# Half of the tokens' turns and squares moved out of a router stage into the matrix product ahead of it

## The chip, the cores and the metric

One NeuronCore of a Trainium2 chip runs the whole program. The metric is the device time of one execution in microseconds (us), as the median of several runs. The engines are named as in the profile: PE (matrix products and transposes through the 128x128 array), PEld (its weight loads), DVE, ACT, POOL and SP, which only issues transfers here.

## The reference

Two model blocks in fp32 for one sequence of 512 tokens behind 16 meta tokens, 528 rows of 1024 columns in all. What matters here is the end of the first block's attention and the routing of its mixture of experts:

```python
mixed = concat(attn, conv)                       # 528 x 1024
h = h + mixed @ w_out                            # "second output product": columns 512 to 1023
hs = rms_norm(h, ffn_norm_g)                     # needs the mean square of each row of h
logits = hs @ w_router                           # 16 experts
aff = softmax(logits)
g, idx = top_k(aff.T, 66)                        # each expert takes its 66 best tokens
y = experts(hs[idx])                             # w_gate, w_up, w_down: 384 MB of weights
h = h.at[idx].add(y * g)
```

The program goes on with a second block of two layers, which the change doesn't touch.

## The kernel before

The program is a row of stages. Each is one block in which every engine has its own instruction list, in order; semaphores order the lists among each other, and all engines meet at the stage's end. Three stages matter.

**The first layer's stage** (`first_layer_stage`) ends with the output product, `out`, a `SplitGemm` of 16 steps (0 to 15). Each step takes 128 rows of `w_out`; steps 0 to 7 make columns 0 to 511 of h, steps 8 to 15 columns 512 to 1023. ACT rounds a weight tile and an activation tile to their high parts (`highs`, L482), DVE subtracts them to get the low parts (`lows`, L495), and PE makes 12 matmuls a step (L429): four tiles of tokens times three products of parts. DVE then adds the four result banks to h (L1320). The fifth tile of tokens has only 16 rows (`tail`); its product runs apart (L986, after steps 7 and 11). Into the same lists are woven, by dictionaries that say "after step s do this", the normalising and turning of the memory rows (`memory_rows`: PE L1473 after steps 6, 8, 10, 12). On PE the last of these follows step 12, and steps 13 to 15 follow without anything between.

**The router stage** (`router_stage`) takes h, five tiles of tokens (`TILES1`: four of 128, one of 16). On PE, `turn(t)` transposes a tile in eight pieces (L1638), `parts(t)` multiplies the turned tile with the weights `gained_w` in 16 narrow matmuls (L1653), and `logits(t)` adds up four partial sums with the table `pick` that POOL makes at the stage's start (L1608 to 1612, L1663). The order on PE is turn(0), then for each t: turn(t+1), logits(t-1), parts(t); ahead of logits(3) stands step 0 of another product, `g` (the memory keys, `mem0`, 16 steps of six matmuls, L429). DVE copies every turned half tile from PSUM (`evict`, L1759) and every partial sum (`take_parts`, L1764), then makes the scaled logits and the softmax (L1772 to 1787) and the choice of 66 tokens (L1790 to 1821). ACT squares h (L1710), takes the root of the sums (L1719), makes the high parts of `g` (`high_of`, L1374), the exponential (L1723), and the normalised rows (`normed`, L1725), which SP stores. POOL makes the low parts of `g` (L1387, a TENSOR_TENSOR on 128x512), and then gathers the first expert's rows (L1622). In `g`'s list on PE, the turned scores (L1670) stand behind step 2 and the turned picks (L1683) behind step 10.

**The experts' stage** multiplies 384 pieces of weights of 1 MB each.

The root, and the exponential that waits for DVE's shifted logits, stand in ACT's list like this:

```python
nc.scalar.activation(ss[:, 1, :], ss[:, 0, :], ACT.Sqrt, ...)   # L1719
for i in range(2, NS): g.high_of(act, i)                        # NS = 6
act.wait_ge(s["shifted"], 1)
nc.scalar.activation(aff[:], aff[:], ACT.Exp)                   # L1723
```

Of the kernel before, what the change touches and what calls it, by code (L numbers as in the profile page):

```python
# [23 lines left out]
P = 128  # L24
D = 1024
# [651 lines left out]

def first_layer_stage(m, tok, hn, qk, v, raw, turns, rot_work, kept, slots, late_slots, mixed, names, at, start_at, scales_at,
                      out_slots, load_early, beside):
# [127 lines left out]
    out_on_tensor, out_on_scalar, out_on_vector = beside  # L807
# [3 lines left out]
    with nc.Block() as block:  # L811
# [25 lines left out]
        def _(pe):  # L837
# [160 lines left out]
            work.setdefault(11, []).append(lambda: tail_products(1))  # L998
            out.products(pe, work, start=3)

        @block.scalar
        def _(act):
# [76 lines left out]
            out.split("act", act, out_on_scalar(act), start=2)  # L1079

        @block.vector
        def _(dve):
# [166 lines left out]
            work = out_on_vector(dve)  # L1249
            work.setdefault(10, []).append(lambda: take_tail(0))  # L1250
# [198 lines left out]
def memory_rows(m, mem_x, mem_split, at):  # L1449
# [70 lines left out]
    return load, on_tensor, on_scalar, on_vector  # L1520
# [12 lines left out]
def router_stage(m, h, w, w_loaded, mem_split, mk_rows, mv, ht, normed, small, slots, first_rows, xg):  # L1533
# [9 lines left out]
    slot = (0, 2, 1, 3, 5)  # L1543
# [26 lines left out]
    junk = m.at("router_junk", [P, D], m.gaps[0])  # L1570
    gained_w = m.area("router_w_gained", [P, KD, 32], 90624)
    PART = (7, 3)
    names = ("w_gained cleared squared root inverse normed turned evicted parts parts_taken tables logits shifted exped "
# [19 lines left out]
    with nc.Block() as block:  # L1593
# [35 lines left out]
        def _(pe):  # L1629
            def turn(t):  # L1630
                n = TILES1[t][1]
                for half in range(2):
                    u = 2 * t + half
                    if u >= 3:
                        pe.wait_ge(s["evicted"], u - 2)
                    for k in range(4):
                        f = 4 * half + k
                        ins = pe.transpose(ps[:, 4 + u % 3, k * P:k * P + n], h[0:n, t, f * P:(f + 1) * P],  # L1638
                                           m.ident[0:n, 0:n])
                    ins.then_inc(s["turned"], 1)  # L1640

            def parts(t):

                t0, n = TILES1[t]
                pe.wait_ge(s["evicted"], 2 * t + 2)
# [4 lines left out]
                for half in range(2):  # L1650
                    for q in range(4):
                        k = 4 * half + q
                        ins = pe.matmul(ps[32 * q:32 * q + 32, PART[t % 2], 0:n], gained_w[:, k, :], ht[:, k, t0:t0 + n],  # L1653
                                        start=(half == 0), stop=(half == 1))
                ins.then_inc(s["parts"], 1)

            def logits(t):
# [3 lines left out]
                if t == 0:  # L1661
                    pe.wait_ge(s["tables"], 1)
                pe.matmul(ps[0:n, 2, slot[t] * NE:(slot[t] + 1) * NE], part[:, t0:t0 + n], pick[:, 0:NE], start=True,  # L1663
# [2287 lines left out]
```

## Time and profile before

| | before |
|---|---|
| median of 3 runs | 2188.51 us (2188.34 to 2189.64) |
| the profiled execution's own time | 2187.14 us |
| its span in the profile | 2185.0 us |
| PE busy | 2156.6 us (99%) |
| DVE, ACT, POOL busy | 1653.7, 1391.6, 337.4 us |
| output product, steps 8 to 15 and what runs beside them | about 238.8 to 265.3 us of the span |
| router stage | 265.8 to about 300.5 us |
| experts' stage | 300.5 to about 1388 us |

The span is what the profile shows of the execution; 2.1 us of the execution's own time lie around it. A matmul's row shows its time from first column to end, and the next one begins before that end, so the distance from start to start is what counts on PE. A `[1.20 <-PEq L811]` behind a row says that the engine sat idle for 1.20 us before it, and what ended that.

### The profile page before, as it was taken

The page shows a single profiled execution, that of the slowest core. Times are in us where ns is not written, and L with a number is a line of the kernel's source. Part 1 is how long each engine was busy: PE and PEld are TensorE (multiplying, and loading weights), DVE is VectorE, ACT ScalarE, POOL GpSimd, SP SyncE. Part 2 cuts the span into 40 slices and gives each one's busy share as a digit, 9 for nine tenths or more (in the row PEclk, how much of TensorE's full clock was granted, in tenths as well). Part 3 has the DMA queues.
Part 4 walks back from the last instruction along what each step waited for, and adds up shares of the span by engine and source line. Part 5 has one row for each costly group of instructions (what it writes and reads, how often), then busy time and mean ns, then how long its engine had stood idle before and what let it go on. Part 6 is the DMA issues. An engine that isn't in the chain of part 4 may idle for free. (4 is left out here: it accounts for less than half of the span.)

```text
span 2185.0 us, 31915 instructions
## 1 busy us (share of the span) xinstructions
PE 2156.6 (99%) x11509; PEld 1556.7 (71%) x11509; DVE 1653.7 (76%) x2157; ACT 1391.6 (64%) x1795; POOL 337.4 (15%) x207
## 2 busy tenths in 40 slices
PE   9999999999999999999999999999999999999999
PEld 9988765565565555555555555687797788888777
DVE  6466678998989989899898898756655556875664
ACT  5345577777777777767777777755555555776653
POOL 3032041211122111121121200330000000211000
PEclk9999999999999999999999999999999999999999
DMA  6213479999999999999999999532221131241301
GB/s 189 84 55 121 166 272 371 376 382 371 387 378 375 381 372 382 386 376 374 373 385 383 374 380 369 207 97 77 83 73 58 58 117 53 61 137 39 116 1 39
DMA packets 179673, 506.88 MB, mean 232 GB/s; under 512 B 12558, under 2 KB 57390, under 8 KB 179582
## 3 DMA queue, kind: packets, MB, share of 16 engines
q1 hardware_dynamic: 174829, 494.92, 60.7%
q0 software_dynamic: 4752, 10.75, 2.2%
q8 instruction: 57, 0.93, 0.2%
q14 instruction: 35, 0.28, 0.0%
HBM read 492.99 MB, written 10.48 MB: 230 GB/s over the span
## 5 line engine op out<-in xcount | busy, mean ns | idle before, releaser
L2249 DVE TENSOR_TENSOR pieces_low<-pieces,pieces_high 128x2048 fp32r<-128x2048 f32 x383 | 873.2, 2289 | 109.4 <-ACT pieces_high L2194 104.8
L2194 ACT ACTIVATE pieces_high<-pieces 128x2048 fp32r<-128x2048 f32 x382 | 729.0, 1916 | 238.3 <-PE ps L2118 231.5
L2118 PE MATMUL ps<-pieces_high,ex_x 128*66 128x512 f32 x2080 | 574.9, 393 | 1.1 <-PEq L1593 0.5
L2118 PEld LDWEIGHTS ps<-pieces_high,ex_x 128*66 128x66 f32 x2080 | 279.4, 136 | 195.3 <-issue 6.9
L2118 PE MATMUL ps<-pieces_low,ex_x 128*66 128x512 f32 x1040 | 323.7, 392 | 0.0
L2118 PE MATMUL ps<-pieces_high,ex_h 128*66 128x512 f32 x992 | 277.3, 393 | 0.0
L495 DVE TENSOR_TENSOR in_w<-ring,in_w 128x256 fp32r<-128x256 f32 (+2 forms) x276 | 124.8, 459 | 155.9 <-ACT in_w L482 154.2
L2585 PE MATMUL ps<-hn_split,in_w 128*128 128x512 f32 x864 | 221.3, 406 | 2.7 <-DVE in_w L495 1.6
L2118 PEld LDWEIGHTS ps<-pieces_low,ex_x 128*66 128x66 f32 x1040 | 141.6, 136 | 97.3
L2118 PEld LDWEIGHTS ps<-pieces_high,ex_h 128*66 128x66 f32 x992 | 133.7, 136 | 90.6 <-DVE pieces_low L2249 3.2
L482 ACT ACTIVATE in_w<-ring 128x256 fp32r<-128x256 f32 (+2 forms) x276 | 117.0, 426 | 126.9 <-PE ps L2585 57.2
L2585 PEld LDWEIGHTS ps<-hn_split,in_w 128*128 128x128 f32 x864 | 159.5, 188 | 44.3 <-DVE in_w L495 5.1
L429 PE MATMUL ps<-out_w,out_a 128*128 128x512 f32 x768 | 180.5, 393 | 2.2 <-DVE out_a L495 1.5
L429 PEld LDWEIGHTS ps<-out_w,out_a 128*128 128x128 f32 x768 | 142.6, 188 | 34.7 <-DVE out_a L495 3.3
L2352 POOL DMA_INDIRECT ex_rows<-xhat_scratch,ex_rows_in x15 | 110.6, 7372 | 320.2 <-DVE ex_rows_in L2255 312.6
L2358 POOL DMA_INDIRECT resid_scratch<-ex_y,ex_rows_out x15 | 73.1, 4871 | 551.8 <-DVE ex_y L2304 551.8
L2118 PE MATMUL ps<-pieces_low,ex_h 128*66 128x512 f32 x496 | 154.4, 392 | 0.0
L2118 PEld LDWEIGHTS ps<-pieces_low,ex_h 128*66 128x66 f32 x496 | 67.6, 136 | 46.9
L495 DVE TENSOR_TENSOR out_w<-ring,out_w 128x512 fp32r<-128x512 f32 x64 | 44.1, 690 | 69.0 <-ACT out_w L482 68.7
L482 ACT ACTIVATE out_w<-ring 128x512 fp32r<-128x512 f32 x64 | 40.2, 628 | 75.2 <-PE ps L429 61.3
L2593 PE MATMUL ps<-in_w,hn_split 128*128 128x256 f32 x576 | 78.5, 289 | 0.0
L3734 POOL TENSOR_TENSOR kn<-kn,k_ss 128x512 f32<-128x512 f32 x8 | 11.1, 1406 | 435.4 <-DVE k_ss L3669 435.4
(510 smaller groups left out, 2772.9 us busy)
## 6 DMA issues: line engine op xcount, KB each, us to landing
pieces<-in_w_gate SPq DMA_DIRECT2D x128, 1024.0 KB, 7.4
pieces<-in_w_up SPq DMA_DIRECT2D x128, 1024.0 KB, 7.7
pieces<-in_w_down SPq DMA_DIRECT2D x128, 1024.0 KB, 8.5
ring<-in_a_w_in SPq DMA_DIRECT2D x24, 1024.0 KB, 5.2
ring<-in_b_w_in SPq DMA_DIRECT2D x4, 2048.0 KB, 7.9
ring<-in_w_in SPq DMA_DIRECT2D x7, 1024.0 KB, 5.0
ring<-in_b_w_out SPq DMA_DIRECT2D x2, 3072.0 KB, 14.4
ring<-in_w_in SPq DMA_DIRECT2D x8, 512.0 KB, 3.6
```

Source lines behind the costliest of these rows:

```text
L429: ins = pe.matmul(self.psum(unit), lhs, rhs, start=(first and i == 0), stop=(last and i == 2))
L482: self.m.nc.scalar.activation(parts[:, 0, :], x, ACT.Copy, scale=scale).then_inc(self.high, 1)
L495: ins = self.m.nc.vector.tensor_tensor(parts[:, 1, :], x, parts[:, 0, :].bitcast(F32), ALU.subtract)
L2118: ins = pe.matmul(ps[0:CAP, banks + c, :], parts[a][:, k0 + k, :], w[b][:, k, c * 512:(c + 1) * 512], start=start and k == 0 and a == b == ...
L2194: nc.scalar.activation(m.high[:, n % NSPLIT, :], m.pieces[:, n % NPIECE, :], ACT.Copy).then_inc(high_done, 1)
L2249: nc.vector.tensor_tensor(m.low_part[:, n % NSPLIT, :], m.pieces[:, n % NPIECE, :], m.high[:, n % NSPLIT, :].bitcast(F32), ALU.subtract).t ...
L2352: nc.gpsimd.indirect_dma_start(out=xg[:], out_offset=None, in_=m.xhat[:], in_offset=bass.IndirectOffsetOnAxis(ap=rows_in[:, 0:1], axis=0)) ...
L2358: nc.gpsimd.indirect_dma_start(out=m.resid[:], out_offset=bass.IndirectOffsetOnAxis(ap=rows_out[:, 0:1], axis=0), in_=y[:], in_offset=None ...
L2585: ins = pe.matmul(psum, w[:, x, u * P:u * P + psum.shape[0]], a[:, y, :], start=(first and i == 0), stop=(last and i == 2))
L2593: ins = pe.matmul(psum[:, b, :], a[:, x, t0:t0 + P], w[:, y, 0:cols], start=(first and i == 0 and b == 0), stop=(last and i == 2 and b == ...
L3734: tt(part, part, spread(r[:, :, h], x.shape[3]), ALU.mult).then_inc(scaled, 1)
```

## The change

Of each tile of tokens, columns 0 to 511 of h are final once the first half of the output product has been added. The change takes the turning and squaring of these halves out of the router stage. On PE, three half tiles (0, 1 and the 16-row tile 4) are turned behind steps 12, 13 and 14, and two (2 and 3) behind step 15, into banks 2, 3, 7, 3, 2. ACT squares the five halves after its own work of steps 12, 13 and 14, each with its row sums into a new tile `half_ss`, and copies three turned halves out of PSUM after that of step 15; it copies the other two at the start of the router stage. DVE clears `half_ss`. In the router only the other halves are turned (PE), copied (DVE, one copy a tile) and squared (ACT). `ht` becomes two tiles, one for each half. DVE adds the two sums of squares, and the root on ACT waits for that sum; of ACT's high parts 2 to 5, which stood behind the root, number 2 goes ahead of it, number 3 stays behind it, and 4 and 5 go behind the exponential. `half_ss` is kept for good, so that every area laid out behind it starts 32 bytes later; two lasting semaphores and two of the stage are new.

```diff
+HALF_SLOT = (0, 2, 1, 3, 5)
+HALF_TURNS = ((0, 2), (1, 3), (len(TILES1) - 1, 7), (2, 3), (3, 2))
+
+
+def turn_half(m, pe, h, i):
+
+    t, bank = HALF_TURNS[i]
+    n = TILES1[t][1]
+    for k in range(4):
+        ins = pe.transpose(m.ps[:, bank, k * P:k * P + n], h[0:n, t, k * P:(k + 1) * P], m.ident[0:n, 0:n])
+    ins.then_inc(m.half_turned, 1)
+
+
+def take_half(m, act, ht0, i):
+
+    t, bank = HALF_TURNS[i]
+    t0, n = TILES1[t]
+    act.wait_ge(m.half_turned, i + 1)
+    m.nc.scalar.activation(ht0[:, :, t0:t0 + n], m.ps[:, bank, :].rearrange("p (k c) -> p k c", k=4)[:, :, 0:n],
+                           ACT.Copy).then_inc(m.half_taken, 1)
...
+    half_junk = m.area("half_junk", [P, 512], 81920)
+    half_cleared, half_squared = m.sem("half_cleared"), m.sem("half_squared")
...
+            def turn_first(i):
+                if i == 0:
+                    pe.wait_ge(out.out["dve"], 4)
+                if i == 2:
+                    pe.wait_ge(tail_taken, 1)
+                    pe.wait_ge(mem_low, KD)
+                if i >= 3:
+                    pe.wait_ge(m.half_taken, 2)
+                turn_half(m, pe, tok, i)
+
+            for i in range(3):
+                work.setdefault(12 + i, []).append(lambda i=i: turn_first(i))
+            work.setdefault(15, []).extend([lambda: turn_first(3), lambda: turn_first(4)])
             out.products(pe, work, start=3)
...
-            out.split("act", act, out_on_scalar(act), start=2)
+
+            def square_first(tiles):
+                act.wait_ge(half_cleared, 1)
+                for t in tiles:
+                    n = TILES1[t][1]
+                    act.wait_ge(*((tail_taken, 1) if t == tail else (out.out["dve"], t + 1)))
+                    nc.scalar.activation(half_junk[0:n, :], tok[0:n, t, 0:512], ACT.Square, scale=D ** -0.5,
+                                         accum_out=m.half_ss[0:n, HALF_SLOT[t]:HALF_SLOT[t] + 1]).then_inc(half_squared, 1)
+                    act.wait_ge(half_squared, t + 1)
+
+            work = out_on_scalar(act)
+            for i, tiles in enumerate(((0, 1), (2, 3), (4,))):
+                work.setdefault(12 + i, []).append(lambda tiles=tiles: square_first(tiles))
+            for i in range(3):
+                work.setdefault(15, []).append(lambda i=i: take_half(m, act, ht0, i))
+            out.split("act", act, work, start=2)
...
+            work.setdefault(8, []).append(lambda: nc.vector.memset(m.half_ss[:], 0.5).then_inc(half_cleared, 1))
...
-    junk = m.at("router_junk", [P, D], m.gaps[0])
+    junk = m.at("router_junk", [P, 512], m.gaps[0])
...
-                for half in range(2):
-                    u = 2 * t + half
-                    if u >= 3:
-                        pe.wait_ge(s["evicted"], u - 2)
-                    for k in range(4):
-                        f = 4 * half + k
-                        ins = pe.transpose(ps[:, 4 + u % 3, k * P:k * P + n], h[0:n, t, f * P:(f + 1) * P],
-                                           m.ident[0:n, 0:n])
-                    ins.then_inc(s["turned"], 1)
+                if t >= 3:
+                    pe.wait_ge(s["evicted"], t - 2)
+                for k in range(4):
+                    ins = pe.transpose(ps[:, 4 + t % 3, k * P:k * P + n], h[0:n, t, (4 + k) * P:(5 + k) * P],
+                                       m.ident[0:n, 0:n])
+                ins.then_inc(s["turned"], 1)
...
-                pe.wait_ge(s["evicted"], 2 * t + 2)
+                pe.wait_ge(s["evicted"], t + 1)
+                if t in (1, 2):
+                    pe.wait_ge(m.half_taken, 4)
+                if t == 3:
+                    pe.wait_ge(m.half_taken, 5)
...
-                        ins = pe.matmul(ps[32 * q:32 * q + 32, PART[t % 2], 0:n], gained_w[:, k, :], ht[:, k, t0:t0 + n],
+                        ins = pe.matmul(ps[32 * q:32 * q + 32, PART[t % 2], 0:n], gained_w[:, k, :], ht[half][:, q, t0:t0 + n],
...
                     pe.wait_ge(s["tables"], 1)
+                    pe.wait_ge(m.half_taken, 5)
...
-                nc.scalar.activation(junk[0:n, :], h[0:n, t, :], ACT.Square, scale=D ** -0.5,
+                nc.scalar.activation(junk[0:n, :], h[0:n, t, 512:D], ACT.Square, scale=D ** -0.5,
                                      accum_out=ss[0:n, 0, slot[t]:slot[t] + 1]).then_inc(s["squared"], 1)
                 act.wait_ge(s["squared"], t + 1)
 
+            for i in (3, 4):
+                take_half(m, act, ht[0], i)
             act.wait_ge(s["cleared"], 1)
             for t in range(nt):
                 square(t)
-                if t >= 2 and t < nt - 1:
-                    g.high_of(act, t - 2)
+                if 1 <= t < nt - 1:
+                    g.high_of(act, t - 1)
+            act.wait_ge(s["sums_added"], 1)
             nc.scalar.activation(ss[:, 1, :], ss[:, 0, :], ACT.Sqrt, bias=m.eps[:, 0:1]).then_inc(s["root"], 1)
-            for i in range(2, NS):
-                g.high_of(act, i)
+            g.high_of(act, 3)
             act.wait_ge(s["shifted"], 1)
             nc.scalar.activation(aff[:], aff[:], ACT.Exp).then_inc(s["exped"], 1)
+            for i in range(4, NS):
+                g.high_of(act, i)
             for t, (_, n) in enumerate(TILES1):
...
-            def evict(u):
-                t, half = divmod(u, 2)
+            def evict(t):
                 t0, n = TILES1[t]
-                dve.wait_ge(s["turned"], u + 1)
-                bank = ps[:, 4 + u % 3, :].rearrange("p (k c) -> p k c", k=4)[:, :, 0:n]
-                nc.vector.tensor_copy(ht[:, 4 * half:4 * half + 4, t0:t0 + n], bank).then_inc(s["evicted"], 1)
+                dve.wait_ge(s["turned"], t + 1)
+                bank = ps[:, 4 + t % 3, :].rearrange("p (k c) -> p k c", k=4)[:, :, 0:n]
+                nc.vector.tensor_copy(ht[1][:, :, t0:t0 + n], bank).then_inc(s["evicted"], 1)
...
-                evict(2 * t)
-                evict(2 * t + 1)
+                evict(t)
                 if t:
                     take_parts(t - 1)
             take_parts(nt - 1)
+            dve.wait_ge(s["squared"], nt)
+            nc.vector.tensor_tensor(ss[:, 0, :], ss[:, 0, :], m.half_ss[:, 0:SLOTS], ALU.add).then_inc(s["sums_added"], 1)
...
+        m.half_ss = m.keep("half_ss", [P, 8])
+        m.half_turned, m.half_taken = m.lasting("half_turned"), m.lasting("half_taken")
         m.arena = m.keep_end
...
+        ht = [m.area(f"h_turned{i}", [P, KD // 2, L1], at) for i, at in enumerate((64512, 40960))]
```

## Rows read from the trace of the kernel before

**Rows 1.** Windows: length, PE, PEld, DVE, ACT, POOL busy us, PEclk, DMA share, GB/s.

```profile
235.70:265.40 29.70, 28.89 (x242) 23.06 (x240) 18.46 (x37) 9.18 (x18) 0.00 (x0) 1.00 0.40 142
...
265.80:275.90 10.10, 9.80 (x137) 8.15 (x137) 7.36 (x20) 9.80 (x18) 6.53 (x17) 1.00 0.93 338
275.90:300.70 24.80, 23.36 (x113) 18.02 (x114) 17.70 (x58) 16.18 (x22) 16.87 (x15) 1.00 0.46 176
300.70:1430.00 1129.30, 1125.16 (x5195) 679.97 (x5196) 1007.00 (x652) 815.39 (x534) 205.97 (x48) 1.00 0.97 366
```

**Rows 2.** Timeline of PE (start us, us, line), second output product and router.

```profile
252.78 3.04 PE L429 MATMUL ps<-out_w,out_a 128*128 128x512 f32 x12
255.66 0.60 PE L1473 MATMUL ps<-masks,mem_x 128*128 128x128 f32 x4
256.01 8.57 PE L429 MATMUL ps<-out_w,out_a 128*128 128x512 f32 x36
265.78 2.07 PE L1638 MATMUL ps<-masks,h 128*128 128x128 f32 x16 [1.20 <-PEq L811]
267.79 0.65 PE L1653 MATMUL ps<-h_turned,router_w_gained 128*32 128x128 f32 x16
268.37 1.10 PE L1638 MATMUL ps<-masks,h 128*128 128x128 f32 x8
269.30 0.29 PE L1663 MATMUL ps<-router_pick,router_part 128*128 128x16 f32 x2
269.52 0.64 PE L1653 MATMUL ps<-h_turned,router_w_gained 128*32 128x128 f32 x16
...
273.32 1.66 PE L429 MATMUL ps<-mem_w,mem_split 128*128 128x512 f32 x6
```

**Rows 3.** Timeline of DVE, the same stretch.

```profile
262.54 2.77 DVE L1320 TENSOR_TENSOR h<-ps,h 128x512 f32<-128x512 f32 x4 [3.80 <-PE ps L429]
...
266.45 2.48 DVE L1759 COPY h_turned<-ps 128x512 f32<-128x512 f32 x4
268.85 0.28 DVE L1764 COPY router_part<-ps 128x128 f32<-128x128 f32 x1
...
275.42 0.17 DVE L1764 COPY router_part<-ps 128x16 f32<-128x16 f32 x1 [1.67 <-PE ps L1653]
...
275.74 0.19 DVE L1774 RECIPROCAL router_ss<-router_ss 128x6 f32<-128x6 f32 x1
...
276.65 1.02 DVE L1782 TENSOR_TENSOR router_aff<-router_aff,router_st 128x96 f32<-128x96 f32 x1
...
278.67 0.28 DVE L1787 TENSOR_TENSOR router_aff<-router_aff,router_st 128x96 f32<-128x96 f32 x1
...
290.31 0.25 DVE L1805 TENSOR_TENSOR router_idxf<-router_found,ps 128x96 f32<-128x96 uint32 x1
```

**Rows 4.** Timeline of POOL, router.

```profile
268.17 0.26 POOL L1612 TENSOR_SCALAR router_pick<-router_pick 128x16 f32<-128x16 f32 x1
...
273.77 5.05 POOL L1387 TENSOR_TENSOR mem_w<-ring,mem_w 128x512 fp32r<-128x512 f32 x4 [0.62 <-ACT mem_w L1374]
279.62 1.29 POOL L1387 TENSOR_TENSOR mem_w<-ring,mem_w 128x512 fp32r<-128x512 f32 x1 [0.79 <-ACT mem_w L1374]
...
285.87 6.29 POOL L1387 TENSOR_TENSOR mem_w<-ring,mem_w 128x512 fp32r<-128x512 f32 x5 [0.27 <-ACT mem_w L1374]
293.66 1.08 POOL L1622 DMA_INDIRECT ex_rows<-xhat_scratch,ex_rows_in  x1 [1.50 <-DVE ex_rows_in L1810]
```

**Rows 5.** Timeline of ACT, router.

```profile
273.08 2.18 ACT L1374 ACTIVATE mem_w<-ring 128x512 fp32r<-128x512 f32 x4
275.27 1.28 ACT L1723 ACT_TABLE_LOAD   x1
277.70 0.28 ACT L1723 ACTIVATE router_aff<-router_aff 128x96 f32<-128x96 f32 x1 [1.14 <-DVE router_aff L1782]
277.89 1.13 ACT L1725 ACTIVATE h_normed<-h,router_ss 128x1024 f32<-128x1024 f32 x1
```

More of the change, by code:

```diff
@@ L675, in last_convolution @@
     return scale, product, add
+HALF_SLOT = (0, 2, 1, 3, 5)
[12 more added lines that the diff above has]
+                           ACT.Copy).then_inc(m.half_taken, 1)
 def first_layer_stage(m, tok, hn, qk, v, raw, turns, rot_work, kept, slots, late_slots, mixed, names, at, start_at, scales_at,
-                      out_slots, load_early, beside):
+                      out_slots, load_early, beside, ht0):
     others = len(m.stage_sems)
@@ L806, in first_layer_stage @@
     tail_out = lambda c, g: ps[32 * g:32 * g + TILES1[tail][1], 4, c * P:(c + 1) * P]
-    out_on_tensor, out_on_scalar, out_on_vector = beside
+    mem_low, out_on_tensor, out_on_scalar, out_on_vector = beside
+    half_junk = m.area("half_junk", [P, 512], 81920)
+    half_cleared, half_squared = m.sem("half_cleared"), m.sem("half_squared")
     o_bank = lambda t: 5 + t % 3
@@ L1518, in on_vector @@
         return work
-    return load, on_tensor, on_scalar, on_vector
+    return load, low, on_tensor, on_scalar, on_vector
 def memory_keys(m, rows, keys, at):
@@ L1542, in router_stage @@
     SLOTS, SEG = 6, 2 * P
-    slot = (0, 2, 1, 3, 5)
+    slot = HALF_SLOT
     at = small
@@ L1569, in router_stage @@
     turned = lambda i: ps[0:CAP, 6, i * NE:(i + 1) * NE]
-    junk = m.at("router_junk", [P, D], m.gaps[0])
+    junk = m.at("router_junk", [P, 512], m.gaps[0])
     gained_w = m.area("router_w_gained", [P, KD, 32], 90624)
     PART = (7, 3)
-    names = ("w_gained cleared squared root inverse normed turned evicted parts parts_taken tables logits shifted exped "
+    names = ("w_gained cleared squared sums_added root inverse normed turned evicted parts parts_taken tables logits shifted exped "
              "weighed turned_scores mine_spread picked picks_turned first_rows picks_taken gather_sent")
@@ L3837, in two_blocks @@
         first_layer_stage(m, h, hn, qk, v, raw, turns, rot_work, kept, m.gaps + [m.arena + work + 8 * L1], late_slots,
-                          hn, names, at + 48 * L1, 20480 + 2 * feat, 24576, spare, load_early, beside)
+                          hn, names, at + 48 * L1, 20480 + 2 * feat, 24576, spare, load_early, beside, ht[0])
         m.close()
@@ L3842, in two_blocks @@
         mv = [m.area(f"mv{l}", [P, 2, 512], 20480 + 8192 * l) for l in range(2)]
-        ht = m.area("h_turned", [P, KD, L1], 40960)
         normed = m.area("h_normed", [P, len(TILES1), D], 57856)
```

## The prediction

> **What bounds the kernel now.** I read the windows first, to see which engine has no time left in each stage. The reader is to see three things in them. In the second output product PE is busy for 28.89 of 29.70 us, with ACT at 9.18: PE sets the pace, and ACT has room [rows 1]. In the router the stage is short of no engine as a whole, but PE and ACT are both busy for 9.80 of its first 10.10 us, and PE's rows there are a chain with DVE's copies [rows 1 to 3]. Behind the router, PE is busy for 1125.16 of 1129.30 us and the transfers fill 0.97 of their engines [rows 1], so nothing behind it can take up a delay or return a gain: a microsecond won or lost ahead of 300.7 us arrives at the end. The granted clock is 1.00, the 2.4 GHz level, in all four windows [rows 1].
>
> Then I read the timelines of the single engines from 252 us to 294 us, to find what waits for what where one stage ends and the next begins. PE's last matmul of the output product ends at 264.58 (256.01 + 8.57) [rows 2], DVE's last addition at 265.31 (262.54 + 2.77) [rows 3], and the router starts on PE at 265.78, 0.47 us later [rows 2]. That start is S below. The router's chain is turn, copy, parts, logits on PE and DVE up to DVE's last copy of a partial sum at 275.42 [rows 3]; that is T, 9.64 us behind S. From T the chain is on DVE and ACT: inverse root at 275.74, shifted logits done at 277.67 (276.65 + 1.02), exponential at 277.70, weights done at 278.95 [rows 3, 5], turned scores, choice, and POOL's gather at 293.66 [rows 4].
>
> **The change part by part: the output product.** It adds 20 transposes to PE where PE is the bound. A step of 12 matmuls takes 8.57 / 3 = 2.86 us at most in the run of 36; from step 12 to step 13 with four transposes of the same shape between are 256.01 - 252.78 = 3.23 us [rows 2]. Four transposes between steps thus cost 0.37 to 0.42 us, and 0.35 where they follow other transposes (255.66 to 256.01) [rows 2]. Half tile 0 follows the memory's transposes: 0.35. Half tile 1: 0.40. Tile 4 has 16 rows and no row of its own beside a product; its bounds are 0.1 (nothing but issue) and 0.42 (as a full one), I take 0.35. So step 15 ends 1.1 us later, and DVE's additions with it. Half tiles 2 and 3 come behind it: in the router eight transposes take 269.30 - 268.37 = 0.93 us [rows 2], so these eight take 0.93 too. They run beside DVE's last addition, which ends 0.73 us behind PE; PE ends up to 0.2 us after it. S moves by 1.1 to 1.3 us; I take **+1.2**.
>
> ACT's additions there (five squares of 512 columns, three copies) lie under PE: ACT is busy 9.18 of 29.70 us [rows 1], some 6 us come to it (eight operations of 0.6 to 0.8), and its high parts are made three steps ahead. Without that cover the whole 6 us would be paid. The new waits on PE (bank free, memory's low parts done, two copies taken by ACT) name things that are done by then, since the banks' first results were added before step 9 and ACT has nothing else to do. What would be queued behind them is only the next step. Nothing is added to SP's list, and its transfers at the router's start move with S.
>
> **The router up to T.** DVE's four copies take 2.48 us, 0.62 each, start to start [rows 3], and parts(0) started 2.01 us behind S (267.79), directly after the second [rows 2, 3]. With one copy before it, it starts at S + 1.39. Between two parts PE spent 269.52 - 267.79 = 1.73 us: 0.58 on parts, 0.93 on eight transposes, 0.22 on logits [rows 2]. Four transposes make it 1.27 us, while DVE needs 0.62 + 0.28 a tile (268.85) [rows 3] and no longer limits. The loop from parts over DVE's copy to logits is near that; I take 1.3 to 1.35. One cover goes: logits(0) needs POOL's table, ready at 268.43 (268.17 + 0.26), S + 2.65 [rows 4]. It was not awaited before (logits(0) at S + 3.52 [rows 2]); now PE comes to it at S + 2.45 and waits 0.3 us, with up to 0.1 more for POOL's clearing of two more semaphores (bounds 0 and 0.4). Parts(1) is then at S + 3.0, parts(2) at 4.4, parts(3) at 5.7, step 0 of `g` at 6.3 instead of 7.54 (273.32) [rows 2]. From there to T the list is unchanged, 2.10 us. T comes at S + 8.35: **-1.3** us, with bounds -1.8 (table and loop free, tail shorter) and -0.9.
>
> ACT's two copies at the start (PSUM, 128x512) end near S + 1.1, ahead of parts(1), the first that needs them. Its five squares are half as long; ACT is at the root by S + 6.4, so it is off this path. Step 0 of `g` needs POOL's first low part. POOL starts it at S + 3.7, and ends after 1.26 (5.05 / 4 [rows 4]): hidden.
>
> **From T to the weights.** The sum of squares can only be added behind DVE's last copy. Before, the root lay ready and DVE went from T to the inverse in 0.32 us. Now: copy 0.14, addition 0.17 (like the copy at 275.42 [rows 3]), then ACT and back. The exponential shows such a round trip: DVE ends at 277.67, ACT starts at 277.70 and takes 0.28 [rows 3, 5], so 0.34. Inverse at T + 0.67: **+0.35**, bounds 0.3 and 0.6.
>
> The next term hangs on a wait that the trace shows once. L1782 took 1.02 us; L1787, the same shape and form, 0.28 [rows 3]. L1782 lay inside POOL's four low parts, whose third ended at 273.77 + 3 x 1.26 = 277.56, and it ended 0.11 later. L1805, which reads one of its inputs from PSUM, took 0.25 inside POOL's run of five [rows 3, 4]. So a DVE operation with both inputs in SBUF that starts inside a POOL low part waits for its end. The Trainium skill, "SBUF — State Buffer", section "Who interferes with whom", says the same of two SBUF inputs and speaks against this change, since it moves low parts beside both operations; by it a wait is at most one POOL instruction.
>
> Where do the low parts go? High part 3 follows the root: ACT at T + 0.54 to 1.1, POOL at T + 1.2 to 2.46. L1782 starts at T + 1.23 + 0.35 = 1.58, inside it, and ends at T + 2.57: again a wait, no term of its own (before T + 2.25, and the 0.35 less 0.03 is counted). The table load of 1.28 us [rows 5] starts at T + 1.05 behind high part 3 and ends at T + 2.33, 0.24 us before it is needed: 0, and 1.3 at most if that cover went. The exponential runs from T + 2.60; the next ACT instruction starts 0.19 later [rows 5], and that is now high part 4, done at T + 3.40 (0.61 long), so that POOL starts low part 4 at T + 3.48. L1787 comes 0.97 us behind the exponential's start (278.67 - 277.70 [rows 3, 5]), at T + 3.57, inside it by 0.09 us. It ends at T + 4.85 and not 3.85: **+1.0**. Low part 4 used to come at 279.62, after L1787 [rows 3, 4]. Bounds 0 (DVE is first) and 1.27.
>
> On the table load page and row differ. The Trainium skill, "ScalarE: Activation LUTs", section "What ACT_TABLE_LOAD costs", gives about 2.66 us with a drain. By that estimate the exponential would wait 1.1 us more; the trace's 1.28 is used.
>
> **After the weights.** `g` has its low parts some 3 us ahead of PE, and the choice on DVE is unchanged. ACT makes two high parts (1.05 us) before the normalised rows. Before, these ended by 285.2 (277.70 + 7.5), 8.5 us ahead of the gather at 293.66 [rows 4, 5]; their stores stay hidden. POOL's last low parts before the gather ended at 292.16 (285.87 + 6.29) [rows 4], some 0.5 us ahead of the chosen rows. They end 1.4 us later against T. With L1787's wait the rows are 1.35 later too, and nothing is added; without it, POOL is late by about 0.4.
>
> The 32 bytes by which later tiles move: no row shows a duration that depends on an address. I take 0; with no row to price it, it only widens the range.
>
> **Sum.** +1.2 - 1.3 + 0.35 + 1.0 = +1.25 us. On the profiled execution's 2187.14 that is 2188.4; that execution lies 1.4 below the median of 2188.51, to which I add the same: **2189.8 us**. A change below 0.2%, 4.4 us, is what a measurement of this kernel can't tell from none.
>
> **The rivals.**
> - *No wait at L1787.* The margin is 0.09 us. Then 1.2 - 1.3 + 0.35 + 0.4 for the late gather = +0.65: 2189.2.
> - *The router gains more.* Tables and loop free (T at -1.8), turns nearly free beside the product (S at +0.9), no wait at L1787 or for POOL: 0.9 - 1.8 + 0.35 = -0.55, and L1782 free would give only 0.2 more, since the table load then sets the exponential (T + 2.33). 2187.8. For it: PE's overlap of short transposes; against: the row of 0.35 in the stream.
> - *The turns are hidden instead of moved*, as the change's form suggests: then S stays, and the sum is +0.05, 2188.6. Against it: PE's 28.89 of 29.70 us [rows 1].
> - *PE's clock falls* (the other side). With 20 transposes less, PE waits more between parts. If the clock went to 1.2 GHz in the router, the 33 us of PE work up to 300.7 [rows 1] would cost up to 33 more; from 4.4 us of work at half clock on it decides. Against it: the clock stayed at 1.00 over an idle time of 1.20 us at the stage's start [rows 1, 2], and the new waits are of 0.3 us. With 10 us of such work: 2199.
>
> **How the numbers follow.** Forecast (wait at L1787) 0.42; no wait 0.28; router gains more 0.10; turns hidden 0.08; clock 0.03; what moved addresses or other spacing in the later stages does, 0.09, of which half is slower by over 4.4 us. All but the last two lie between 2187 and 2191. The sum's own bounds (S 0.2, T 0.4, L1787 1.0) and the runs' spread of 1.3 us give 2186.5 to 2192.2. Faster 0.03, same 0.89, slower 0.08.
>
> **What would show it.** After the change: step 15 ends 1.1 us later on PE; the router's first row comes 1.2 later; T is 8.35 behind it; the root stands on ACT behind DVE's addition; L1787 takes 1.2 us or more; the experts start about 1.25 us later, at 302. The prediction is wrong if the experts start more than 3 us from 300.7, or if they don't and the end moves anyway: then it is the later stages.

## The result and the profile after

| | before | after |
|---|---|---|
| median | 2188.34 us (14 runs, 2186.99 to 2190.03) | 2193.53 us (14 runs, 2191.64 to 2195.25) |
| ratio | | 1.0023, 95% interval 1.0016 to 1.0030 |
| profiled execution's own time, span | 2187.14, 2185.0 us | 2192.17, 2190.0 us |

The change costs 5.2 us, where +1.3 was forecast and 2192.2 was the upper end of the range. PE's timeline of the changed kernel, where that of before is [rows 2]:

```profile
253.52 3.03 PE L429 MATMUL ps<-out_w,out_a 128*128 128x512 f32 x12
...
256.83 0.60 PE L687 MATMUL ps<-masks,h 128*128 128x128 f32 x4
257.19 3.02 PE L429 MATMUL ps<-out_w,out_a 128*128 128x512 f32 x12
260.04 0.60 PE L687 MATMUL ps<-masks,h 128*128 128x128 f32 x4
260.39 3.02 PE L429 MATMUL ps<-out_w,out_a 128*128 128x512 f32 x12
263.35 0.41 PE L687 MATMUL ps<-masks,h 16*128 16x16 f32 x4
263.69 3.04 PE L429 MATMUL ps<-out_w,out_a 128*128 128x512 f32 x12
266.57 1.03 PE L687 MATMUL ps<-masks,h 128*128 128x128 f32 x8
267.93 1.06 PE L1689 MATMUL ps<-masks,h 128*128 128x128 f32 x8 [0.32 <-PEq L835]
269.34 0.64 PE L1708 MATMUL ps<-h_turned,router_w_gained 128*32 128x128 f32 x16 [0.35 <-DVE h_turned L1818]
...
281.56 0.51 PE L1726 MATMUL ps<-masks,router_aff 128*32 128x128 f32 x3 [1.60 <-DVE router_aff L1847]
...
303.10 0.66 PE L2178 MATMUL ps<-pieces_high,ex_x 128*66 128x512 f32 x2 [0.50 <-PEq L1647]
```

The first row is step 12: it starts at 253.52, 0.74 us later than before, although nothing ahead of it was edited but the clearing of the new tile on DVE and the places of tiles (this doesn't stand out: in the profiles of the other seven kernels that leave the areas ahead of it in place, experiments 2 and 5 to 10, the same row starts at 252.86 to 253.43; in experiment 1, where they are moved, at 253.81). From there the three inserted turns are seen (L687), and step 15 ends at 263.69 + 3.04 = 266.73 us. DVE and the other two engines, where those of before are [rows 3 to 5]:

```profile
264.69 2.77 DVE L1374 TENSOR_TENSOR h<-ps,h 128x512 f32<-128x512 f32 x4 [5.16 <-PE ps L429]
...
276.56 0.17 DVE L1823 COPY router_part<-ps 128x16 f32<-128x16 f32 x1 [1.68 <-PE ps L1708]
276.65 0.15 DVE L1831 TENSOR_TENSOR router_ss<-router_ss,half_ss 128x6 f32<-128x6 f32 x1
...
277.30 0.19 DVE L1834 RECIPROCAL router_ss<-router_ss 128x6 f32<-128x6 f32 x1 [0.39 <-ACT router_ss L1778]
...
278.20 1.00 DVE L1842 TENSOR_TENSOR router_aff<-router_aff,router_st 128x96 f32<-128x96 f32 x1
...
280.21 1.29 DVE L1847 TENSOR_TENSOR router_aff<-router_aff,router_st 128x96 f32<-128x96 f32 x1
```

```profile
277.80 1.29 POOL L1441 TENSOR_TENSOR mem_w<-ring,mem_w 128x512 fp32r<-128x512 f32 x1 [2.39 <-ACT mem_w L1428]
280.12 5.02 POOL L1441 TENSOR_TENSOR mem_w<-ring,mem_w 128x512 fp32r<-128x512 f32 x4 [1.03 <-ACT mem_w L1428]
```

```profile
276.90 0.30 ACT L1778 ACTIVATE router_ss<-router_ss,eps 128x6 f32<-128x6 f32 x1 [2.72 <-DVE router_ss L1831]
...
277.74 1.28 ACT L1781 ACT_TABLE_LOAD   x1
279.24 0.28 ACT L1781 ACTIVATE router_aff<-router_aff 128x96 f32<-128x96 f32 x1 [0.22 <-DVE router_aff L1842]
```

The reader is to see three waits. The root on ACT (L1778) starts at 276.90, as soon as DVE's addition of the sums (L1831, 276.65) has landed. L1842, formerly L1782, ends at 279.20, 0.11 us behind POOL's low part of 277.80 to 279.09, as its forerunner did. L1847, formerly L1787, starts at 280.21, 0.09 us behind the start of POOL's next low parts (280.12), and takes 1.29 us instead of 0.28: it ends at 281.50, again 0.1 us behind the end of the first of them (280.12 + 5.02 / 4 = 281.37; T is 276.56 here). PE waits 1.60 us for it.

The whole difference of the spans, 5.0 us, by stretches:

| stretch | before | after | difference | forecast |
|---|---|---|---|---|
| 0 to start of step 12 | 252.78 | 253.52 | +0.74 | 0 |
| step 12 to DVE's last addition | 12.53 | 13.94 | +1.41 | +1.2 |
| router's first DVE row to T (last copy of a partial sum) | 9.60 | 8.59 | -1.01 | -1.3 |
| T to the turned scores on PE | 3.58 | 5.00 | +1.42 | +1.35 |
| turned scores to the experts' first product | 21.72 | 21.54 | -0.18 | 0 |
| experts' first product to the end | 1884.28 | 1886.90 | +2.62 | 0 |

The four middle rows, which the change edits, sum to 1.64 us; the first and the last, which it doesn't edit, to 3.36. In the experts' stage the delay is no step. Each of the 16 experts makes its hidden layer in two halves, 32 in all. ACT's activation of the second hidden half (ex_hidden), and the same instruction 30 halves on, before and after:

```profile
346.49 1.02 ACT L2200 ACTIVATE ex_hidden<-ps 66x1024 f32<-66x1024 f32 x1 [0.82 <-PE ps L2118]
...
1365.59 1.02 ACT L2200 ACTIVATE ex_hidden<-ps 66x1024 f32<-66x1024 f32 x1 [0.74 <-PE ps L2118]
```

```profile
348.94 1.02 ACT L2260 ACTIVATE ex_hidden<-ps 66x1024 f32<-66x1024 f32 x1 [0.86 <-PE ps L2178]
...
1369.99 1.02 ACT L2260 ACTIVATE ex_hidden<-ps 66x1024 f32<-66x1024 f32 x1 [0.78 <-PE ps L2178]
```

These are 1019.10 and 1021.05 us for the same 30 half experts, 0.065 us more for each, and between them the delay grows evenly. PE is busy throughout. The page's groups of the experts' products, before and after (mean ns of one in the last column before the idle time):

```profile
L2118 PE MATMUL ps<-pieces_high,ex_x 128*66 128x512 f32 x2080 | 574.9, 393 | 1.1 <-PEq L1593 0.5
...
L2118 PE MATMUL ps<-pieces_low,ex_x 128*66 128x512 f32 x1040 | 323.7, 392 | 0.0
L2118 PE MATMUL ps<-pieces_high,ex_h 128*66 128x512 f32 x992 | 277.3, 393 | 0.0
...
L2118 PE MATMUL ps<-pieces_low,ex_h 128*66 128x512 f32 x496 | 154.4, 392 | 0.0
```

```profile
L2178 PE MATMUL ps<-pieces_high,ex_x 128*66 128x512 f32 x2080 | 576.6, 394 | 0.9 <-PEq L1647 0.5
...
L2178 PE MATMUL ps<-pieces_low,ex_x 128*66 128x512 f32 x1040 | 324.2, 393 | 0.0
L2178 PE MATMUL ps<-pieces_high,ex_h 128*66 128x512 f32 x992 | 276.5, 393 | 0.0
...
L2178 PE MATMUL ps<-pieces_low,ex_h 128*66 128x512 f32 x496 | 154.8, 393 | 0.0
```

A matmul that has ex_x or the low ex_h as its weights takes 0.5 to 0.8 ns longer (busy time over count), and the page's whole numbers just show it; one with the high ex_h takes 0.8 ns less (276.5 for 277.3 us of busy time over 992).

### The profile page after: what moved, and what is told of

Same layout as the page of the kernel before. It is cut to its first block and busy times, and to the rows that moved or that the text cites. A ratio compares the mean times of both kernels' runs of the same rounds, so it can differ in the third digit from the quotient of the medians.

```text
span 2190.0 us, 31941 instructions
## 1 busy us (share of the span) xinstructions
PE 2161.4 (99%) x11509; PEld 1557.5 (71%) x11509; DVE 1653.0 (75%) x2154; ACT 1395.7 (64%) x1810; POOL 337.2 (15%) x207
## 5 line engine op out<-in xcount | busy, mean ns | idle before, releaser
L2178 PE MATMUL ps<-pieces_high,ex_x 128*66 128x512 f32 x2080 | 576.6, 394 | 0.9 <-PEq L1647 0.5
L2178 PE MATMUL ps<-pieces_low,ex_x 128*66 128x512 f32 x1040 | 324.2, 393 | 0.0
L2178 PE MATMUL ps<-pieces_high,ex_h 128*66 128x512 f32 x992 | 276.5, 393 | 0.0
L2178 PE MATMUL ps<-pieces_low,ex_h 128*66 128x512 f32 x496 | 154.8, 393 | 0.0
```

What stands on the lines that cost most here:

```text
L2178: ins = pe.matmul(ps[0:CAP, banks + c, :], parts[a][:, k0 + k, :], w[b][:, k, c * 512:(c + 1) * 512], start=start and k == 0 and a == b == ...
```

## The experiments

Two theories were put against each other. A: the move of every area by 32 bytes slows instructions in stages that the change doesn't edit. B: the slowdown comes from the other additions (semaphores, longer lists, the new timing of the router).

**1. The kernel before, only moved.**

```diff
         m.rows = m.keep("rows", [CAP, NE + 1], U32)
+        m.keep("pad", [P, 8])
```

> The kernel before, with nothing added but an unused kept tile of 32 bytes, so that every area starts 32 bytes later, as in the changed kernel. Theory A (the addresses cause what the router doesn't explain): about 3.5 us slower than before, ratio 1.0016, spread over all stages, the experts' stage some 2 us longer. Theory B (it is the other additions: semaphores, longer lists, the timing of the router): same as before within 0.5 us.

Measured: 2191.69 us against 2188.04, ratio 1.0016 (1.0007 to 1.0025), +3.65 us. The 30 halves:

```profile
347.60 1.02 ACT L2200 ACTIVATE ex_hidden<-ps 66x1024 f32<-66x1024 f32 x1 [0.86 <-PE ps L2118]
...
1368.52 1.02 ACT L2200 ACTIVATE ex_hidden<-ps 66x1024 f32<-66x1024 f32 x1 [0.78 <-PE ps L2118]
```

That is 1020.92 us, 1.82 more than before, with no edited instruction at all. Theory A holds. Its profile is 4.6 us longer than that of before: 1.0 of it ahead of step 12, where kernels that were not moved differ by 0.65 too, 1.8 in the 30 halves, and 1.6 behind the last half.

**2. The changed kernel, not moved.** The sums lie in the 28 unused bytes behind eps.

```diff
-        self.eps = self.keep("eps", [P, 1])
+        eps_row = self.keep("eps", [P, 8])
+        self.eps, self.half_ss = eps_row[:, 0:1], eps_row[:, 1:8]
...
-        m.half_ss = m.keep("half_ss", [P, 8])
```

> The changed kernel with the sums of squares put into the unused bytes behind the small constant eps, so that no area moves. Theory A: 1.6 us slower than before (the local sum of output product and router), 3.5 us faster than the changed kernel. Theory B: 5 us slower than before, as the changed kernel. In both the profile shows the experts' first product about 1.6 to 2.4 us later than before.

Measured: 2190.09 against 2188.04, ratio 1.0010 (1.0001 to 1.0019), +2.05 us. The 30 halves take 1019.16 us, as before, and the groups are back at their old means but for 394 in one, whose busy time, 277.3 us, is that of before:

```profile
349.42 1.02 ACT L2261 ACTIVATE ex_hidden<-ps 66x1024 f32<-66x1024 f32 x1 [0.82 <-PE ps L2179]
...
1368.58 1.02 ACT L2261 ACTIVATE ex_hidden<-ps 66x1024 f32<-66x1024 f32 x1 [0.74 <-PE ps L2179]
```

```profile
L2179 PE MATMUL ps<-pieces_high,ex_x 128*66 128x512 f32 x2080 | 575.0, 393 | 1.0 <-PEq L1648 0.5
...
L2179 PE MATMUL ps<-pieces_low,ex_h 128*66 128x512 f32 x496 | 154.4, 392 | 0.0
```

The experts' first product comes at 303.62, 2.90 us later than before, where at most 2.4 was expected; the clock fell for a short time behind the turned scores, which took 1.2 us of this (see the last rival below). So the change's own edits cost about 2 us, and the rest of the 5.2 goes with the addresses.

**3. The changed kernel, moved by 64 bytes.**

```diff
-        m.half_ss = m.keep("half_ss", [P, 8])
+        m.half_ss = m.keep("half_ss", [P, 16])
```

> The changed kernel with 64 instead of 32 bytes kept for the sums, so that every area moves by 64. Theory A, if it is the place within 64 bytes that counts: 1.6 us slower than before. Theory A, if any move counts (256-byte places): about 5 us slower. Theory B: 5 us slower, as the changed kernel.

Measured: 2191.07 against 2188.04 (1.0015, 1.0006 to 1.0024), +3.0 us, with runs from 2188.2 to 2194.1. The 30 halves take 1020.82 us (348.44 to 1369.26), 1.7 more than before: the experts' stage pays for a move by 64 too. What the whole run pays is not shown. The median is 1.0 above that of experiment 2, with intervals that overlap, and the profile gives the time back: from the last half's activation (1369.26) to the span's end (2186.1) are 816.8 us, against 819.4 before and 819.3 in experiment 2.

**4. The changed kernel, moved by 128 bytes.**

```diff
-        m.half_ss = m.keep("half_ss", [P, 8])
+        m.half_ss = m.keep("half_ss", [P, 32])
```

> The changed kernel with 128 bytes kept for the sums, so that every area moves by 128 instead of 32. If the cost of the addresses goes by their place within 128 bytes, it is gone: 1.6 to 2.0 us slower than before, and no drift in the experts' stage. If any move costs: 3 to 5 us slower.

Measured: 2193.37 against 2188.36 (1.0024, 1.0015 to 1.0034), +5.0 us; 1021.82 us for the 30 halves (349.66 to 1371.48), the longest of all. Of the 5.0 the change's own edits are 2 (experiment 2), and the clock fell for a short time twice in this profile, outside the 30 halves (means of 0.88 over 281 to 295 us and over 1580 to 1594 us). The place within 32, 64 or 128 bytes is thus not what decides; my expectation that 128 might be free fell.

**5. The kernel before, only PE's weights of the experts moved.** The tiles ex_x and ex_h (and the scaled rows, which PE doesn't read) are moved by 32 bytes, all else stays.

```diff
-    h_part = [m.area(f"ex_h{i}", [P, KD, CAP], at + size * (2 + i), F32R) for i in range(2)]
+    h_part = [m.area(f"ex_h{i}", [P, KD, CAP], at + 32 + size * (2 + i), F32R) for i in range(2)]
...
-        m.x_tiles = ([m.area(f"ex_x{i}", [P, KD, CAP], 74752 + size * i, F32R) for i in range(2)],
-                     m.area("ex_x_scaled", [P, KD, CAP], 74752 + 4 * size))
+        m.x_tiles = ([m.area(f"ex_x{i}", [P, KD, CAP], 74784 + size * i, F32R) for i in range(2)],
+                     m.area("ex_x_scaled", [P, KD, CAP], 74784 + 4 * size))
```

> The kernel before with only the five tiles of the experts' split and scaled rows moved by 32 bytes (they are PE's stationary operands there), all else in place. If these tiles carry the drift of the experts' stage: that stage 1.8 us longer, the rest unchanged, 1.8 us slower than before (2189.9). If it is other tiles, or any other property of the moved kernel: same as before within 0.4 us.

Measured: 2190.16 against 2188.36 (1.0009, 1.0000 to 1.0018), +1.8 us, as expected, though the interval just reaches 1. The 30 halves and the groups:

```profile
347.14 1.02 ACT L2200 ACTIVATE ex_hidden<-ps 66x1024 f32<-66x1024 f32 x1 [0.86 <-PE ps L2118]
...
1368.35 1.02 ACT L2200 ACTIVATE ex_hidden<-ps 66x1024 f32<-66x1024 f32 x1 [0.78 <-PE ps L2118]
```

```profile
L2118 PE MATMUL ps<-pieces_high,ex_x 128*66 128x512 f32 x2080 | 576.3, 394 | 0.9 <-PEq L1593 0.5
...
L2118 PE MATMUL ps<-pieces_low,ex_x 128*66 128x512 f32 x1040 | 324.2, 393 | 0.0
L2118 PE MATMUL ps<-pieces_high,ex_h 128*66 128x512 f32 x992 | 276.5, 393 | 0.0
...
L2118 PE MATMUL ps<-pieces_low,ex_h 128*66 128x512 f32 x496 | 154.8, 393 | 0.0
```

1021.21 us, and the busy times of the changed kernel to within 0.3 us in every group (576.3 for 576.6, 324.2, 276.5, 154.8).

**6. The wait of DVE for POOL, taken away in the changed kernel.** In the kernel of experiment 2, ACT makes high parts 4 and 5 behind the first normalised tile.

```diff
-            for i in range(4, NS):
-                g.high_of(act, i)
             for t, (_, n) in enumerate(TILES1):
                 nc.scalar.activation(normed[0:n, t, :], ...)
+                if t == 0:
+                    for i in range(4, NS):
+                        g.high_of(act, i)
```

> As the changed kernel without the move of areas, and with high parts 4 and 5 on ACT behind the first normalised tile instead of ahead of it, so that POOL's low part 4 starts behind DVE's L1787 operation. If DVE waits for POOL there, that operation takes 0.28 us instead of 1.29, the turned scores come 1.0 us earlier relative to T, and the run is 1.0 us faster than the same kernel without the reordering (0.6 if POOL's last low parts then hold up the gather). If that wait is not POOL's doing, the operation still takes 1.29 us and nothing is gained.

```profile
277.67 1.00 DVE L1844 TENSOR_TENSOR router_aff<-router_aff,router_st 128x96 f32<-128x96 f32 x1
...
279.68 0.26 DVE L1849 TENSOR_TENSOR router_aff<-router_aff,router_st 128x96 f32<-128x96 f32 x1
```

The second operation now takes 0.26 us and not 1.29, the first still 1.00. The turned scores come at T + 3.96 instead of 5.00. Measured 2189.59 against 2188.04 (1.0007, 0.9998 to 1.0016): 0.5 us faster than experiment 2 by the medians, which differ by less than their intervals, so the 1.0 that was expected of the run is shown by the trace alone.

**7. The same idea in the kernel before.** High parts 2 and 3 stay behind the root, 4 and 5 go behind the first normalised tile.

```diff
-            for i in range(2, NS):
+            for i in range(2, 4):
                 g.high_of(act, i)
...
+                if t == 0:
+                    for i in range(4, NS):
+                        g.high_of(act, i)
```

> The kernel before with high parts 4 and 5 moved on ACT from behind the root to behind the first normalised tile, so that POOL is free when DVE's L1782 operation starts. If that operation waits for POOL: it takes 0.28 instead of 1.02 us, and the run is 0.74 us faster than before (2187.3). If not: the same.

```profile
277.08 0.26 DVE L1785 TENSOR_TENSOR router_aff<-router_aff,router_st 128x96 f32<-128x96 f32 x1
...
278.35 0.26 DVE L1790 TENSOR_TENSOR router_aff<-router_aff,router_st 128x96 f32<-128x96 f32 x1
```

```profile
276.23 3.06 PE L429 MATMUL ps<-mem_w,mem_split 128*128 128x512 f32 x12
279.12 0.50 PE L1670 MATMUL ps<-masks,router_aff 128*32 128x128 f32 x3
```

L1782's operation (here L1785) falls from 1.02 to 0.26 us. The turned scores come at T + 3.26 and not T + 2.84, because PE is now still at steps 1 and 2 of `g` (276.23 to about 279.1): 0.32 us are gained and not 0.74. Measured 2187.11 against 2188.36 (0.9997, 0.9988 to 1.0006): 1.25 faster in the median, not by more than the interval, and the trace accounts for 0.3 of it.

**8. Both waits gone in the changed kernel.** Experiment 6, with high part 3 ahead of the root as well.

```diff
+            g.high_of(act, 3)
             act.wait_ge(s["sums_added"], 1)
...
-            g.high_of(act, 3)
```

> The changed kernel without the move of areas, high part 3 ahead of ACT's wait for the sums, and 4 and 5 behind the first normalised tile, so that neither DVE operation meets a POOL low part. Both take 0.28 us; the turned scores come at T + 3.2 instead of 5.0. Against the same kernel with only 4 and 5 moved: 0.7 us faster, so 0.8 us slower than before (2188.9).

Measured 2188.49 against 2188.36 (0.9999, 0.9990 to 1.0008). The turned scores come at T + 3.27. So the best form of the change that was found is level with the kernel before, and by the medians 1.4 us above the kernel before with the same reordering.

**9. Only ex_h moved by 32 bytes**, on top of experiment 7.

```diff
-    h_part = [m.area(f"ex_h{i}", [P, KD, CAP], at + size * (2 + i), F32R) for i in range(2)]
+    h_part = [m.area(f"ex_h{i}", [P, KD, CAP], at + 32 + size * (2 + i), F32R) for i in range(2)]
...
-                     m.area("ex_x_scaled", [P, KD, CAP], 74752 + 4 * size))
+                     m.area("ex_x_scaled", [P, KD, CAP], 74784 + 4 * size))
```

> The reordered kernel before (high parts 4 and 5 moved) with only the experts' hidden split tiles ex_h (and the scaled rows, which PE doesn't read) moved by 32 bytes; ex_x stays. If each tile's address sets the distance between PE's matmuls on its own: products with ex_h as high part fall from 231.3 to 230.5 ns and those with ex_h and the low pieces rise from 230.3 to 231.2, as when all five tiles moved, those with ex_x keep 230.8 and 230.1 ns; the experts' stage is 0.4 us shorter, the run 1.6 us faster than before. If the effect is one of the whole arrangement: the ex_x products change too.

```profile
L2121 PE MATMUL ps<-pieces_high,ex_x 128*66 128x512 f32 x2080 | 575.0, 393 | 1.0 <-PEq L1593 0.5
...
L2121 PE MATMUL ps<-pieces_low,ex_x 128*66 128x512 f32 x1040 | 323.8, 392 | 0.0
L2121 PE MATMUL ps<-pieces_high,ex_h 128*66 128x512 f32 x992 | 276.2, 392 | 0.0
...
L2121 PE MATMUL ps<-pieces_low,ex_h 128*66 128x512 f32 x496 | 154.9, 393 | 0.0
```

The groups of ex_x stay at 393 and 392, those of ex_h go to 392 and 393. The 30 halves take 1018.64 us (346.82 to 1365.46), against 1018.84 in experiment 7: 0.2 less, where 0.4 was expected. The run itself, 2188.11 against 2187.68 (0.9999, 0.9990 to 1.0008), says nothing of it; the 1.6 us that it was to be faster are not seen, nor is the gain of experiment 7 that they rested on. The profiled execution is the slowest of its runs, 2194.83 us; its granted clock is 1.00 over the 30 halves and falls only behind them (a mean of 0.96 over 1366 to 1500 us).

**10. Only the high tile of ex_h at a place 32 bytes off**, behind the scaled rows; these and the low tile lie one tile earlier.

```diff
-    h_part = [m.area(f"ex_h{i}", [P, KD, CAP], at + size * (2 + i), F32R) for i in range(2)]
+    h_part = [m.area(f"ex_h{i}", [P, KD, CAP], at + (32 + size * 4 if i == 0 else size * 2), F32R) for i in range(2)]
...
-                     m.area("ex_x_scaled", [P, KD, CAP], 74752 + 4 * size))
+                     m.area("ex_x_scaled", [P, KD, CAP], 74752 + 3 * size))
```

> The same, with only the high tile of the hidden part at a place 32 bytes off (behind the others), its low tile and the scaled rows one tile size earlier. By single addresses, with ex_x untouched: experts' stage 0.8 to 1.2 us shorter, the run about 2 us faster than before (2186.3). If it is the whole arrangement: anything between 1.5 us shorter and 2 us longer.

Measured: 2188.49 against 2187.68 (1.0003, 0.9994 to 1.0012). The 30 halves take 1020.10 us (346.19 to 1366.29), 1.3 more than in experiment 7. If each tile's address acted by what had been seen before, 0.8 to 1.2 less were expected; the result lies in the range of the other case, the whole arrangement.

**What the two say together.** The distance from one start to the next tells it more finely than the busy times. Means in ns over the records of each trace between 340 and 1340 us, distances over 300 left out; the numbers at the head are the experiments, of which 1, 3 and 4 and the changed kernel move all areas:

```
weights, pieces   before  changed  1       3       4       5        7        9        10
                          by 32    by 32   by 64   by 128  (ex_x,   (none    (ex_h    (high ex_h
                                                           ex_h)    moved)   moved)   elsewhere)
ex_x, high        230.78  231.65   231.61  231.34  231.99  231.55   230.76   230.76   230.99
ex_x, low         230.09  230.60   230.55  230.18  230.90  230.70   229.95   230.15   230.20
ex_h, high        231.31  230.44   230.48  232.84  230.68  230.45   230.97   230.14   231.84
ex_h, low         230.29  231.16   231.15  231.52  230.43  231.18   230.05   231.15   230.86
```

In experiments 2, 6 and 8, where the kernel is the changed one and no tile is moved, the four are 230.69 to 230.81, 230.03 to 230.08, 231.37 to 231.40 and 230.22 to 230.29, as before. A tile at the same place has the same distance to within 0.45 ns in all these kernels, whether the router is changed or not. Moved by 32 bytes, ex_x and the low ex_h become slower by 0.5 to 1.1 and the high ex_h faster by 0.8 to 0.9. At other places the same tile can go the other way: the high ex_h is slower when moved by 64 (232.84) and in experiment 10 (231.84). So the place counts, and no rule for it was found. Nor is it shown whether it is the place by itself: the pieces, PE's other operand, lie ahead of the kept tiles and stayed still in every run, so each move also changed the place of the weights against them.

**The runs sorted by their clock.** Each run lists its mean granted clock, and at 0.998 the medians are 1.0 to 2.9 us above those at 1.000, in every kernel but that of experiment 4, which has one run at 1.000 (0.2). Medians of the runs at 1.000 alone, against those of the kernel before in the same comparison (number of runs in brackets):

```
                                   us           before        difference
1  before, all moved by 32         2190.1 (3)   2187.3 (15)   +2.9
2  changed, not moved              2189.1 (2)   2187.3 (15)   +1.8
3  changed, moved by 64            2188.2 (1)   2187.3 (15)   +1.0
4  changed, moved by 128           2193.2 (1)   2187.8 (13)   +5.3
5  before, ex_x and ex_h moved     2189.4 (5)   2187.8 (13)   +1.6
6  changed, not moved, reordered   2188.4 (2)   2187.3 (15)   +1.1
7  before, reordered               2186.7 (6)   2187.8 (13)   -1.1
8  as 6, and part 3 moved up       2187.4 (4)   2187.8 (13)   -0.5
9  as 7, ex_h moved                2186.5 (3)   2187.3 (8)    -0.8
10 as 7, high ex_h elsewhere       2187.9 (4)   2187.3 (8)    +0.6
```

The changed kernel has 2192.3 there (4 runs): some 4.5 to 5.0 above, and 2.9 + 1.8 = 4.7. The runs are few, but the two halves add up. Beside experiment 2's 1.8, a move by 64 costs nothing here (3) and one by 128 costs 3.5 (4), each by a single run.

## Why the prediction was wrong

The step that failed is "The 32 bytes by which later tiles move: no row shows a duration that depends on an address. I take 0". It was right about the rows at hand, and the sum took their silence for a zero. The move of all areas costs 3.65 us by experiment 1 (the changed kernel differs from experiment 2 by 3.1; 2.9 with the clock at 1.000), of which PE's weights in the experts' stage make 1.8 (experiment 5; 1.6 at 1.000). The other 1.3 to 1.9 lie in tiles that were not moved singly; which of them carry it stays open. The prediction gave this 0.09 and no price, and its range ended 1.3 us below the median. A price could have been had from rows: PE sets the pace for nearly the whole span, so 1 ns on each of some 11,500 matmuls is 11 us. The forecast's own sign of this came: the experts start at 303.1, within 3 us of 300.7, and the end moved by 5.

The other points, by their own steps:

- *Output product, +1.2.* Measured +1.41, over its bound of 1.3. From start to start of the steps on PE (before, from the single records in the run of 36; now, the rows above), step 12 takes 3.67 us for 3.23, step 13 3.20 for 2.87, step 14 3.30 for 2.77, and step 15 to its end 3.04 for 2.93. So half tile 0 cost 0.44 (0.35 forecast), half tile 1 0.34 (0.40), the 16-row tile, mis-sized most, 0.53 (0.35), and step 15 behind it 0.11. That is 1.4 where 1.1 was taken. The two turns behind step 15, priced at 0 to 0.2, cost nothing: they end at 267.60 on PE, DVE's addition at 267.46, and the router starts 0.5 us behind DVE as before.
- *The turns are hidden*, the rival: wrong, by the same rows.
- *Router up to T, -1.3.* Measured -1.01. Parts(0) starts at S + 1.41 (1.39 forecast), logits(0) at S + 2.89 (2.8), kept back by POOL's table; the loop from parts to parts takes 1.38 to 1.39 us (271.11, 272.50, 273.88 on PE), where 1.3 to 1.35 was taken. S here is 267.93, PE's first row of the router, and T comes 8.63 us behind it (8.35 forecast).
- *The root's round trip, +0.35.* Measured 277.30 - 276.56 = 0.74 against 0.32: +0.42.
- *The wait at L1787, +1.0.* Right, by a margin as narrow as it was said to be: start forecast at T + 3.57, seen at T + 3.65; 0.09 us behind POOL's start, as forecast. The Trainium skill, "SBUF — State Buffer", section "Who interferes with whom", calls this the lock of the shared port by whichever starts first, and experiments 6 and 7 agree: without a POOL operation beside it, the same DVE operation takes 0.26 us. One reading in the working was wrong, and the sum didn't hang on it: the low part at 279.62 is number 6, not 4. Numbers 4 and 5 were the last two of the run of four and ended at 278.82 (273.77 + 5.05), 0.15 us behind L1787's start, which is why it lost almost nothing then.
- *L1782 costs nothing more; the table load is hidden.* Right: the load ends at 279.02 and the exponential starts at 279.24. The Trainium skill, "ScalarE: Activation LUTs", section "What ACT_TABLE_LOAD costs", gives about 2.66 us with the drain, which would have ended it at 280.4. The trace has the load's own 1.28 us and no drain: the exponential starts 0.22 us behind the load, as soon as DVE is done.
- *After the weights.* Right, -0.18 us: from the gather on POOL to PE's first use of its rows are 4.22 us (296.21 to 300.43) instead of 4.40.
- *PE's clock falls*, the rival. In the profile of the changed kernel it doesn't. In two of the four profiles that have the 1.6 us wait of PE (experiments 2 and 4) it does, right behind it. The same window of experiment 2 and of the changed kernel (columns as in [rows 1]: window, its length, busy us of PE, PEld, DVE, ACT and POOL with their instructions, granted clock, DMA share, GB/s):

```profile
281.00:295.00 14.00, 14.00 (x64) 11.29 (x63) 10.68 (x36) 12.13 (x17) 12.33 (x10) 0.88 0.47 184
```

```profile
281.00:295.00 14.00, 13.34 (x66) 10.61 (x67) 11.63 (x40) 13.22 (x19) 13.03 (x11) 1.00 0.53 207
```

The mean of 0.88 is a short time at the 1.2 GHz level in 14 us. Experiment 2's 48 matmuls there took 12.86 us, against 11.34 in the changed kernel: 1.5 us, not the 10 of the rival. In the eight profiles without that wait the clock held at this place. That the wait brings it on is likely, not shown.

The sum of the edited parts, 1.64 us in the trace and 2.05 by the medians of experiment 2, stands against the forecast of 1.25. The forecast would have been within its range (2190.1 by experiment 2) if the tile had been put into unused bytes.

## What to carry to other kernels

Where one engine sets the pace of a long kernel, any edit that moves its operands in memory is an edit of every stage: put a new tile where it moves nothing, or measure the old kernel with the same move, before a difference of a few tenths of a per cent is put down to the edit. Work moved from one stretch in which PE sets the pace into another in which it does too is not hidden; here it cost 1.4 us there and saved 1.0. Before reordering, lay DVE's operations with two SBUF inputs beside POOL's list: a POOL operation that started 0.09 us earlier cost 1.0 us here, nearly its whole length.

## What the runs showed of the hardware that was not expected

The distance between two matmuls on 128x512 in the experts' stage of this kernel depends on where the tile of weights lies, by 1 to 2 ns in 230, and does so the same way in every kernel that has the tile at the same place. With the areas moved by 32, 64 and 128 bytes, the 30 halves took 1.7 to 2.7 us longer; moving ex_h alone by 32 shortened them by 0.2, and moving the high one of its tiles to another place lengthened them by 1.3. A move can also give time back: by 64 bytes, the part behind the last half took 816.8 us and not 819.4, in the one profile of it. Whether it is the loading of the weights, the product, their place against the pieces, or something that meets them, no run here tells apart.
